# Feed-forward blocks that end by token half, and the norm behind them taken half by half

## The chip, the cores and the metric

One core of a Trainium2 chip runs the whole program. The metric is the time of one launch on the device, in microseconds; the kernel before was run three times, with a median of 3149.17 us (3148.85 to 3149.45). Besides, one execution was taken by the hardware profiler.

## The reference, cut to what matters

The model is a stack of layers on 256 tokens of width 1024. Two layers with a mixture of experts come first, then four layers whose second half is a plain feed-forward block. What is computed around the change is this, four times:

```python
def _layernorm(x, g, b):
    mu = mean(x); var = mean((x - mu) ** 2)
    return (x - mu) * rsqrt(var + eps) * g + b

def _swiglu(x, w_gate_up, w_down):           # hidden width 2816
    gate, up = split(x @ w_gate_up, 2)
    return (silu(gate) * up) @ w_down

for i in range(4):
    h = mixer_i(x)                            # HGRN, mLSTM, S5, HGRN
    x = _layernorm(ALPHA_2 * x + h, ...)
    x = _layernorm(ALPHA_2 * x + _swiglu(x, ...), ...)
```

A norm is taken over the 1024 values of one token. So the norm of the first 128 tokens needs nothing of the other 128.

## The kernel before, in words

Each engine has its own program, written out in order, and the engines meet at semaphores. The residual `h` lies in SBUF as two halves of 128 tokens (`t` = 0, 1), each of two column halves of 512 (`c` or `q` = 0, 1). `acc` is four PSUM banks, two for each token half: banks 4 and 5 for the first, 6 and 7 for the second. Before a feed-forward block, `residual_pe` has put the scaled residual there.

**The feed-forward block** (`glu_pe`, L559) has 11 parts of 256 hidden channels. For each part `glu_pe_up` (matmuls of L536 and L537) makes the gate and the up projection. ACT and DVE then make the hidden values of the part (`glu_act_step`, `glu_dve_step`): ACT copies the low product of "up" (L608), DVE adds it (L623), multiplies (L626), casts (L628) and takes the low part (L630), which announces `glu_hid_done`. Then `glu_pe_down` (L540, matmuls of L552) adds the part's product with the down weights to `acc`: 24 matmuls, 12 for the first token half and then 12 for the second. The hidden values are the operand that is loaded as weights. The down product of a part runs on PE one step late, behind the next part's up products, so that the hidden values are made under it. At the end, PE does up(10), down(9), down(10). In down(10) the first half's 12th matmul announces `glu_first_sum`, and the last matmul `glu_down_done`. The weights come through a ring of 12 slots that SP fills in order; a slot is loaded again when its use is announced.

**The norm behind it** is number 5, 7, 9 and 11 (`ln_dve`, L439, with `ALPHA` already in). DVE takes the statistics of the first half as soon as `glu_first_sum` is there (two of L452, then L455 and L457), then those of the second half when `glu_down_done` is there. ACT takes a square root for each half (`ln_act`, L475). Only then does DVE apply the norm: for each half a reciprocal (L462) and, for each column half, L465 and L468, the second of which announces `ln_done`.

**What follows norms 5, 7 and 9** is `turn_pe` (L361): four calls of a filler matmul on an idle operand (`keep_busy`, L359, two records each), then for each of the four pieces of `h` four transposes (L377) as soon as its `ln_done` is there, then five calls more of the filler. ACT copies each transposed piece (L407), but in its program this comes behind both square roots; DVE takes the low parts (L418, four), but behind the whole norm. Then ACT and DVE split the first two weight units of the next stage in the same way (L281 on ACT, then L286 on DVE), and PE begins the next projection: L2475 (the mLSTM's gates) behind norm 5, L312 behind norms 7 and 9. Behind norm 11 comes only the store of `h`.

Of the kernel before, what the change touches and what calls it, by code (L numbers as in the profile page):

```python
# [26 lines left out]
ALU = mybir.AluOpType  # L27
# [5 lines left out]
TT = T // P  # L33
# [61 lines left out]
def build(nc, W, out):  # L95

    ctx = ExitStack()
    with ctx:
# [3 lines left out]
        def sem(name):  # L102

            if name not in sems:
                sems[name] = ctx.enter_context(nc.semaphore(name))
            return sems[name]

        def sb(name, shape, dt=F32):
            return ctx.enter_context(nc.sbuf_tensor(name, shape, dt))

        def done(name):

            counts[name] = counts.get(name, 0) + 1
            return counts[name]


        act_step, dve_step, pool_step = sem("act_step"), sem("dve_step"), sem("pool_step")
        act_steps, dve_steps, pool_steps = Count(), Count(), Count()
# [6 lines left out]
        acc = psum[:, 4:8, :].rearrange("p (t b) n -> p t (b n)", t=TT)  # L125
# [43 lines left out]
        h = sb("h", [P, TT, D])  # L169
        ln_gb = scratch[:, SCR - 1, :].rearrange("p (k d) -> p k d", k=2)  # L170
# [57 lines left out]
        def slot_r(n):  # L228
            return ring_r[n % RING][:, :]
# [197 lines left out]
        mean_var = small[:, 24:28].rearrange("p (t s) -> p t s", t=TT)  # L427
        ln_sd = small[:, 28:30]
        ln_rstd = small[:, 30:32]
# [6 lines left out]
            pool.dma_start(ln_gb[:, 0, :], g.partition_broadcast(P)).then_inc(sem("ln_params_landed"), 16)  # L436
            pool.dma_start(ln_gb[:, 1, :], b.partition_broadcast(P)).then_inc(sem("ln_params_landed"), 16)

        def ln_dve(dve, n, alpha, wait_mix, mix=acc, by_tile=True):  # L439


            v = dve
            halves = [slice(c * 512, (c + 1) * 512) for c in range(2)]
            y = mix if alpha is None else h
            for t, c in [(t, c) for t in range(TT) for c in range(2)] if by_tile else [(t, c) for c in range(2) for t in range(TT)]:
                wait_mix(dve, t, c)
                x = y[:, t, halves[c]]
                if alpha is not None:
                    v.scalar_tensor_tensor(out=x, in0=x, scalar=alpha, in1=mix[:, t, halves[c]],
                                           op0=ALU.mult, op1=ALU.add).then_inc(dve_step, 1)  # L450
                    dve.wait_ge(dve_step, dve_steps.next())
                v.bn_stats(bn_s[:, t, c, :], x).then_inc(dve_step, 1)  # L452
                dve.wait_ge(dve_step, dve_steps.next())
                if c == 1:
                    v.bn_aggr(mean_var[:, t, :], bn_s[:, t, :, :]).then_inc(dve_step, 1)  # L455
                    dve.wait_ge(dve_step, dve_steps.next())
                    v.tensor_scalar(mean_var[:, t, 1:2], mean_var[:, t, 1:2], LN_EPS, None, ALU.add).then_inc(sem("ln_var"), 1)  # L457
                    dve.wait_ge(sem("ln_var"), done("ln_var"))
            dve.wait_ge(sem("ln_params_landed"), 32 * (n + 1))
            for t in range(TT):  # L460
                dve.wait_ge(sem("ln_sd_done"), 2 * n + t + 1)
                v.reciprocal(ln_rstd[:, t:t + 1], ln_sd[:, t:t + 1]).then_inc(dve_step, 1)  # L462
                dve.wait_ge(dve_step, dve_steps.next())
                for x in halves:
                    v.scalar_tensor_tensor(out=h[:, t, x], in0=y[:, t, x], scalar=mean_var[:, t, 0:1], in1=ln_gb[:, 0, x],  # L465
                                           op0=ALU.subtract, op1=ALU.mult).then_inc(dve_step, 1)
                    dve.wait_ge(dve_step, dve_steps.next())
                    v.scalar_tensor_tensor(out=h[:, t, x], in0=h[:, t, x], scalar=ln_rstd[:, t:t + 1], in1=ln_gb[:, 1, x],  # L468
                                           op0=ALU.mult, op1=ALU.add).then_inc(sem("ln_done"), 1)
                    dve.wait_ge(sem("ln_done"), done("ln_done"))  # L470

        def ln_act(act, n):
            for t in range(TT):
# [63 lines left out]
                        mm = pe.matmul(bank[:, 0:T], w[1][:, j, fc], both[:, 0, j, :], start=False, stop=(j == KT - 1))  # L537
                mm.then_inc(sem(name), 1)

        def glu_pe_down(pe, g, s, i=0):  # L540

            step = i * SLOTS + s
            pe.wait_ge(sem("glu_hid_done"), step + (g.g0 + 1))
            n, _ = g.unit("down", s, i)
            pe.wait_ge(sem("glu_down_split"), step + (g.g0 + 1))
            w = [x.rearrange("p (f n) -> p f n", f=FT) for x in (glu_hi["down"][s % 2], slot_r(n))]
            hid = [x.rearrange("p (f t) -> p f t", f=FT) for x in (hid_hi[s % 2], hid_lo[s % 2])]
            for t in range(TT):
                for c in range(2):
                    for f in range(FT):  # L550
                        for x, a in PASSES:
                            mm = pe.matmul(acc[:, t, c * 512:(c + 1) * 512], hid[x][:, f, t * P:(t + 1) * P],  # L552
                                           w[a][:, f, c * 512:(c + 1) * 512],
                                           start=False, stop=(s == g.n - 1 and f == FT - 1 and x == 1))
                if t == 0 and isinstance(s, int) and s == g.n - 1:
                    mm.then_inc(sem("glu_first_sum"), 1)
            mm.then_inc(sem("glu_down_done"), 1)

        def glu_pe(pe, g):  # L559
            glu_pe_up(pe, g, 0)  # L560
            glu_pe_up(pe, g, 1)
            glu_pe_down(pe, g, 0)
            with pe.Fori(0, g.loops) as i:
                for k in range(SLOTS):
                    glu_pe_up(pe, g, 2 + k, i)
                    glu_pe_down(pe, g, 1 + k, i)
            for s in range(2 + SLOTS * g.loops, g.n):
                glu_pe_up(pe, g, s)
                glu_pe_down(pe, g, s - 1)
            glu_pe_down(pe, g, g.n - 1)  # L570

        USED = {"gate": "glu_gate_ready", "up": "glu_up_ready", "down": "glu_down_done"}

# [73 lines left out]
        def glu_ahead_dve(dve, g):  # L647
            glu_low(dve, g, "gate", 0)
            glu_low(dve, g, "up", 0)
# [7 lines left out]
        def wait_glu(g):  # L657
            def wait(dve, t, c):
                if c == 0 and t == 0:
                    dve.wait_ge(sem("glu_first_sum"), g.nth + 1)  # L660
                elif c == 0:
                    dve.wait_ge(sem("glu_down_done"), g.g0 + g.n)
            return wait
# [1281 lines left out]
        def wait_experts(g):  # L1945
            return lambda dve, t, c: dve.wait_ge(sem("experts_done"), TT * g.layer + t + 1)
# [1230 lines left out]
        ffn = [None] * 4  # L3177
# [38 lines left out]
        def wait_out(stage):  # L3216
            return lambda dve, t, c: dve.wait_ge(sem(OUT_UNIT), plan[stage][1] - 2 + 2 * c)
# [126 lines left out]
        @block.vector  # L3344
        def _(dve):
            turn_parts_dve(dve, 0)
            dn_dve(dve)
            ln_dve(dve, 0, ALPHA_FIRST, wait_out("dn_out"), by_tile=False)
            route_dve(dve, 0)
            experts_dve(dve, moe[0])  # L3350
            ln_dve(dve, 1, None, wait_experts(moe[0]))
            turn_parts_dve(dve, 2)
            da_dve(dve)
            ln_dve(dve, 2, ALPHA_FIRST, wait_out("da_out"), by_tile=False)
            route_dve(dve, 1)
            experts_dve(dve, moe[1])
            ln_dve(dve, 3, None, wait_experts(moe[1]))
            turn_parts_dve(dve, HG_LN[0])
            hg_dve(dve, 0)
            glu_ahead_dve(dve, ffn[0])  # L3360
            ln_dve(dve, 4, ALPHA_SECOND, wait_out("hg0_out"), by_tile=False)
            turn_parts_dve(dve, 5)
            glu_dve(dve, ffn[0])
            ln_dve(dve, 5, None, wait_glu(ffn[0]))
            turn_parts_dve(dve, ML_TURN)
            ml_dve(dve)
            glu_ahead_dve(dve, ffn[1])
            ln_dve(dve, 6, ALPHA_SECOND, wait_out("ml_out"), by_tile=False)
            turn_parts_dve(dve, 7)
            glu_dve(dve, ffn[1])  # L3370
            ln_dve(dve, 7, None, wait_glu(ffn[1]))
            turn_parts_dve(dve, S5_TURN)
            s5_dve(dve)
            glu_ahead_dve(dve, ffn[2])
            ln_dve(dve, 8, ALPHA_SECOND, s5_mix_dve, s5_mix, by_tile=False)
            turn_parts_dve(dve, 9)
            glu_dve(dve, ffn[2])
            ln_dve(dve, 9, None, wait_glu(ffn[2]))
            turn_parts_dve(dve, HG_LN[1])
            hg_dve(dve, 1)  # L3380
            glu_ahead_dve(dve, ffn[3])
            ln_dve(dve, 10, ALPHA_SECOND, wait_out("hg1_out"), by_tile=False)
            turn_parts_dve(dve, 11)
            glu_dve(dve, ffn[3])
            ln_dve(dve, 11, None, wait_glu(ffn[3]))


# [14 lines left out]
```

## Time and profile before

| | us |
|---|---|
| median of 3 runs | 3149.17 (3148.85 to 3149.45) |
| the profiled execution's own time | 3146.78 |
| its span | 3145.2 |
| PE busy (matmul), DVE busy, ACT busy | 2857.0, 1557.1, 906.5 |
| granted TensorE clock, mean | 0.957 of full speed |

The span is the time from the first to the last instruction in the trace. Busy time is the sum of an engine's instructions; matmuls are pipelined, so PE is busy on paper also where matmuls overlap. The engines work side by side, so only what lies on the chain that ends last sets the time.

### The profile page before, as it was taken

To read this page: it belongs to the slowest core of one execution; us is meant where nothing else is said; L and a number is where in the kernel's file an instruction comes from. 1 tells how busy PE (TensorE), PEld (TensorE's weight loads), DVE (VectorE), ACT (ScalarE), POOL (GpSimd) and SP (SyncE) were. 2 spreads that over 40 slices of the span, in tenths; PEclk is the share of its full clock that TensorE was granted. 3 is DMA by queue.
4 is the path that set the end of the run, shared out by engine and by line. 5 is a ranking of instruction groups with operands and counts; after the bars stand their busy time and mean duration, and the time that the engine had idled before them with its cause. 6 is when DMAs were issued, how large, how long until landed. Compare 5 with 4: busy or idle time off the path is not lost.

```text
span 3145.2 us, 41647 instructions
## 1 busy us (share of the span) xinstructions
PE 2857.0 (91%) x16772; PEld 2103.6 (67%) x16774; DVE 1557.1 (50%) x2133; ACT 906.5 (29%) x1016; POOL 217.7 (7%) x309
## 2 busy tenths in 40 slices
PE   8888999998969999998898999999968899988998
PEld 8786444444846444443687887878856878787887
DVE  7855111111664111111576665675589576567664
ACT  4522110101431110110433443344330344333442
POOL 2001000000000000000021000000066000002000
PEclk9998999999978999999999999999978999999999
DMA  9204899999415999999432554345520245532450
GB/s 306 94 1 161 360 422 422 422 422 396 163 51 220 422 422 422 422 422 398 144 106 94 174 187 141 121 145 188 188 68 1 99 160 187 150 128 81 148 188 26
DMA packets 274118, 681.86 MB, mean 217 GB/s; under 512 B 10984, under 2 KB 207856, under 8 KB 223296
## 3 DMA queue, kind: packets, MB, share of 16 engines
q1 hardware_dynamic: 266080, 639.79, 54.8%
q0 software_dynamic: 7904, 40.19, 3.5%
q8 instruction: 96, 1.57, 0.2%
q14 instruction: 38, 0.31, 0.0%
HBM read 678.88 MB, written 1.05 MB: 216 GB/s over the span
## 4 chain that ended last, share of the span: by engine, by line
PE 60%; DVE 18%; DMA 17%; issue 2%; ACT 2%; SPq 0%; POOL 0%; DVEq 0%; ACTq 0%; POOLq 0%
DMA ring<-moe_w 16%; PE psum L536 11%; PE psum L1646 8%; PE psum L552 8%; PE psum L537 5%; PE psum L325 5%; PE psum L336 5%; PE psum L312 4%; PE psum L1671 3%; DVE ring_r L286 2%; PE psum L2210 1%; PE psum L1629 1%; DVE scratch L808 1%; PE psum L359 1%; DVE h L468 1%
## 5 line engine op out<-in xcount | busy, mean ns | idle before, releaser
L536 PE MATMUL psum<-scratch_r,scratch_r 128*128 128x512 f32 x1408 | 498.7, 398 | 1.7 <-DVE scratch_r L418 1.6
L1646 PE MATMUL psum<-ring,scratch 128*64 128x512 f32 x2016 | 450.2, 595 | 43.2 <-DMA ring<-moe_w 43.1
L537 PE MATMUL psum<-scratch_r,ring_r 128*128 128x256 f32 x1408 | 395.1, 281 | 0.0
L1646 PEld LDWEIGHTS psum<-ring,scratch 128*64 128x64 f32 x2016 | 146.6, 137 | 320.9 <-issue 317.0
L536 PEld LDWEIGHTS psum<-scratch_r,scratch_r 128*128 128x128 f32 x1408 | 264.5, 188 | 70.1 <-DVE scratch_r L418 5.0
L588 DVE TENSOR_TENSOR ring_r<-ring,scratch_r 128x2048 fp32r<-128x2048 f32 x132 | 294.8, 2286 | 19.4 <-ACT scratch_r L581 19.2
L286 DVE TENSOR_TENSOR ring_r<-ring,scratch_r 128x2048 fp32r<-128x2048 f32 x88 | 203.6, 2321 | 172.3 <-ACT scratch_r L281 171.0
L1845 DVE SCALAR_TENSOR_TENSOR hT_r<-psum,small,hT_r 128x512 fp32r<-128x512 f32 x66 | 46.5, 746 | 453.5 <-ACT hT_r L1784 453.5
L537 PEld LDWEIGHTS psum<-scratch_r,ring_r 128*128 128x128 f32 x1408 | 265.8, 189 | 1.4
L581 ACT CAST scratch_r<-ring 128x2048 fp32r<-128x2048 f32 x132 | 247.1, 1912 | 60.4 <-PE psum L552 60.2
L552 PE MATMUL psum<-scratch_r 128*128 128x512 f32 x704 | 225.2, 392 | 0.0
L312 PE MATMUL psum<-scratch_r,scratch_r 128*128 128x256 f32 x896 | 206.5, 288 | 8.3 <-DVE ring_r L286 8.3
L1671 PE MATMUL psum<-ring,scratch 128*64 128x512 f32 x960 | 211.1, 592 | 0.0
L281 ACT CAST scratch_r<-ring 128x2048 fp32r<-128x2048 f32 x88 | 166.8, 1903 | 104.0 <-PE psum L336 86.5
L1784 ACT ACTIVATE hT_r<-psum,small 128x512 fp32r<-128x512 f32 x66 | 41.7, 683 | 430.4 <-PE psum L1671 430.4
L312 PEld LDWEIGHTS psum<-scratch_r,scratch_r 128*128 128x128 f32 x896 | 157.2, 196 | 10.3 <-issue 10.3
L1671 PEld LDWEIGHTS psum<-ring,scratch 128*64 128x64 f32 x960 | 68.9, 137 | 137.0 <-issue 137.0
L1827 DVE TENSOR_TENSOR scratch<-scratch,psum 128x512 f32<-128x512 f32 x33 | 22.7, 688 | 265.7 <-ACT scratch L1777 265.7
L552 PEld LDWEIGHTS psum<-scratch_r 128*128 128x128 f32 x704 | 132.1, 188 | 29.3
L312 PE MATMUL psum<-hT_r,scratch_r 128*128 128x256 f32 x448 | 129.6, 289 | 16.1 <-DVE ring_r L286 15.2
L336 PE MATMUL psum<-scratch_r 128*128 128x256 f32 x448 | 121.0, 299 | 24.8 <-DVE scratch_r L903 19.1
L552 PE MATMUL psum<-ring_r,scratch_r 128*128 128x512 f32 x352 | 137.2, 390 | 0.0
(522 smaller groups left out, 4890.9 us busy)
## 6 DMA issues: line engine op xcount, KB each, us to landing
ring<-moe_w SPq DMA_DIRECT2D x372, 1024.0 KB, 20.5
ring<-ffn_w_gate_up SPq DMA_DIRECT2D x88, 1024.0 KB, 5.1
ring<-ffn_w_down SPq DMA_DIRECT2D x44, 1024.0 KB, 4.9
ring<-hgrn_w_in SPq DMA_DIRECT2D x32, 1024.0 KB, 5.5
scratch<-moe_w POOLq DMA_DIRECT2D x24, 1024.0 KB, 11.2
ring<-a_w_in SPq DMA_DIRECT2D x16, 1024.0 KB, 12.8
ring<-mlstm_w_in SPq DMA_DIRECT2D x12, 1024.0 KB, 5.2
ring<-kv_w SPq DMA_DIRECT2D x8, 1024.0 KB, 11.9
```

Source lines behind the costliest of these rows:

```text
L281: act.copy(hi, slot(n)).then_inc(sem("unit_high"), 1)
L286: dve.tensor_tensor(slot_r(n), slot(n), hi, ALU.subtract).then_inc(sem("unit_split"), 1)
L312: mm = pe.matmul(bank[:, c, :], w[:, j, c * P:(c + 1) * P], x[:, j, :], start=(j == 0 and m == 0), stop=(j == KT - 1 and m == len(terms) - 1))
L325: mm = pe.matmul(bank[:, t, :], x[:, j, t * P:(t + 1) * P], w[:, j, :], start=(j == 0 and m == 0), stop=(j == KT - 1 and m == len(terms) - 1))
L336: mm = pe.matmul(acc[:, t, i * COLS:(i + 1) * COLS], x[:, j, t * P:(t + 1) * P], w[:, j, :], start=(j == 0 and m == 0), stop=(j == KT - 1 ...
L536: pe.matmul(bank, w[0][:, j, fc], both[:, :, j, :], start=(j == 0), stop=False)
L537: mm = pe.matmul(bank[:, 0:T], w[1][:, j, fc], both[:, 0, j, :], start=False, stop=(j == KT - 1))
L552: mm = pe.matmul(acc[:, t, c * 512:(c + 1) * 512], hid[x][:, f, t * P:(t + 1) * P], w[a][:, f, c * 512:(c + 1) * 512], start=False, stop=( ...
L581: act.copy(glu_hi[kind][s % 2], slot(n)).then_inc(sem(f"glu_{kind}_high"), 1)
L588: dve.tensor_tensor(slot_r(n), slot(n), glu_hi[kind][s % 2], ALU.subtract).then_inc(sem(f"glu_{kind}_split"), 1)
L1646: mm = pe.matmul(psum[c, k, :], xg[:, j, c], ws[x][:, i, k, :], start=(j == 0), stop=(j == KT - 1))
L1671: mm = pe.matmul(psum[c, 2 + b, :], moe_hidT[:, 2 * half + a, c], ws[x][:, a, b * 512:(b + 1) * 512], start=(half == 0 and a == 0), stop=( ...
```

## The change

In all four feed-forward blocks PE no longer does the last two down products one behind the other. It does down(9) and down(10) for the first token half, then down(9) and down(10) for the second. `glu_pe_down` gets an argument `of` for this; it waits for the hidden values and the split weights at each call, as before. `glu_down_done` is announced once for each part, behind its second half. The norm's function is cut in two, and with `apart=True` (norms 5, 7, 9 and 11 only) DVE does statistics and application of the first half, then statistics and application of the second. No instruction that computes is added or removed, and ACT's program is unchanged.

```diff
-        def ln_dve(dve, n, alpha, wait_mix, mix=acc, by_tile=True):
+        def ln_dve(dve, n, alpha, wait_mix, mix=acc, by_tile=True, apart=False):
+            if apart:
+                for t in range(TT):
+                    ln_stats_dve(dve, n, alpha, wait_mix, mix, [(t, c) for c in range(2)])
+                    if t == 0:
+                        dve.wait_ge(sem("ln_params_landed"), 32 * (n + 1))
+                    ln_apply_dve(dve, n, mix if alpha is None else h, t)
+                return
...
-        def glu_pe_down(pe, g, s, i=0):
+        def glu_pe_down(pe, g, s, i=0, of=range(TT)):
...
-            for t in range(TT):
+            for t in of:
...
-            mm.then_inc(sem("glu_down_done"), 1)
+            if TT - 1 in of:
+                mm.then_inc(sem("glu_down_done"), 1)
...
             for s in range(2 + SLOTS * g.loops, g.n):
                 glu_pe_up(pe, g, s)
-                glu_pe_down(pe, g, s - 1)
-            glu_pe_down(pe, g, g.n - 1)
+                if s < g.n - 1:
+                    glu_pe_down(pe, g, s - 1)
+            for t in range(TT):
+                for s in (g.n - 2, g.n - 1):
+                    glu_pe_down(pe, g, s, of=(t,))
...
-            ln_dve(dve, 5, None, wait_glu(ffn[0]))
+            ln_dve(dve, 5, None, wait_glu(ffn[0]), apart=True)
```

`ln_stats_dve` and `ln_apply_dve` hold the instructions of the old body unchanged; norms 7, 9 and 11 are called in the same way.

## Rows read from the trace of the kernel before

**Rows 1.** The page: the chain that ended last, shares of the span by engine.

```profile
PE 60%; DVE 18%; DMA 17%; issue 2%; ACT 2%; SPq 0%; POOL 0%; DVEq 0%; ACTq 0%; POOLq 0%
```

**Rows 2.** Chain of waits behind block 0: start us, us, what.

```profile
1914.89 5.23 PE psum L552 x23
...
1929.48 5.99 PE psum L359 x10
1935.47 5.47 PE psum L2475 x48
```

**Rows 3.** Timeline of DVE, last block: start us, us, engine line op out<-in xcount [idle].

```profile
3123.78 0.69 DVE L630 TENSOR_TENSOR scratch_r<-scratch,scratch_r 128x512 fp32r<-128x512 f32 x1
3129.40 1.43 DVE L452 BATCH_NORM_STATS2 small<-psum 128x6 f32<-128x512 f32 x2 [4.93 <-PE psum L552]
...
3132.19 1.43 DVE L452 BATCH_NORM_STATS2 small<-psum 128x6 f32<-128x512 f32 x2 [0.92 <-PE psum L552]
...
3133.90 0.15 DVE L457 TENSOR_SCALAR small<-small 128x1 f32<-128x1 f32 x1
3134.09 0.16 DVE L462 RECIPROCAL small<-small 128x1 f32<-128x1 f32 x1
...
3136.64 0.75 DVE L468 SCALAR_TENSOR_TENSOR h<-h,small,scratch 128x512 f32<-128x512 f32 x1
...
3139.99 0.75 DVE L468 SCALAR_TENSOR_TENSOR h<-h,small,scratch 128x512 f32<-128x512 f32 x1
```

**Rows 4.** Timeline of ACT, last block.

```profile
3134.14 0.20 ACT L475 ACTIVATE small<-small 128x1 f32<-128x1 f32 x1 [2.64 <-DVE small L457]
```

**Rows 5.** Timeline of PE, last block's two down products.

```profile
3120.98 0.40 PE L552 MATMUL psum<-scratch_r 128*128 128x512 f32 x1
...
3123.53 0.61 PE L552 MATMUL psum<-scratch_r 128*128 128x512 f32 x2
...
3128.97 0.61 PE L552 MATMUL psum<-scratch_r 128*128 128x512 f32 x2
...
3131.70 0.39 PE L552 MATMUL psum<-scratch_r 128*128 128x512 f32 x1
```

**Rows 6.** Timeline of PE and DVE where PE waits for an operand (behind norm 6).

```profile
2087.90 2.87 DVE L418 TENSOR_TENSOR scratch_r<-psum,scratch_r 128x512 fp32r<-128x512 f32 x4
...
2090.82 0.50 PE L536 MATMUL psum<-scratch_r,scratch_r 128*128 128x512 f32 x1 [0.53 <-DVE scratch_r L418]
...
2091.16 0.28 PE L537 MATMUL psum<-scratch_r,ring_r 128*128 128x256 f32 x1
```

**Rows 7.** Timeline of PE behind norm 5.

```profile
1919.94 3.59 PE L359 MATMUL psum<-ident 128*128 128x512 f32 x8
...
1929.31 6.15 PE L359 MATMUL psum<-ident 128*128 128x512 f32 x10
```

**Rows 8.** Timeline of PE and DVE behind norm 7.

```profile
2284.50 1.12 PE L377 MATMUL psum<-ident,h 128*128 128x128 f32 x4 [0.92 <-DVE h L468]
...
2288.33 2.29 DVE L286 TENSOR_TENSOR ring_r<-ring,scratch_r 128x2048 fp32r<-128x2048 f32 x1 [0.98 <-ACT scratch_r L281]
```

**Rows 9.** Timeline of PE and DVE behind norm 9.

```profile
2729.59 1.12 PE L377 MATMUL psum<-ident,h 128*128 128x128 f32 x4 [0.61 <-DVE h L468]
...
2733.41 4.49 DVE L286 TENSOR_TENSOR ring_r<-ring,scratch_r 128x2048 fp32r<-128x2048 f32 x2 [0.98 <-ACT scratch_r L281]
...
2736.65 0.68 PE L312 MATMUL psum<-scratch_r,scratch_r 128*128 128x256 f32 x1
```

**Rows 10.** Windows: us, busy and count of PE, PEld, DVE, ACT, POOL; PEclk, DMA share, GB/s.

```profile
2082.40:2085.10 2.70, 1.27 (x10) 0.94 (x10) 2.56 (x5) 0.58 (x1) 0.00 (x0) 1.00 0.00 0
1923.50:1929.50 6.00, 2.69 (x18) 1.94 (x18) 5.71 (x9) 1.76 (x3) 0.44 (x1) 1.00 0.21 71
1929.30:1931.30 2.00, 2.00 (x5) 0.88 (x4) 1.90 (x4) 1.70 (x3) 0.52 (x3) 0.55 0.45 158
```

**Rows 11.** Timeline of SP's DMA issues.

```profile
1903.54 16.96 SPq L679 DMA_DIRECT2D ring<-mlstm_w_in  x4
```

More of the change, by code:

```diff
@@ L437, in ln_params, with ln_stats_dve @@
             pool.dma_start(ln_gb[:, 1, :], b.partition_broadcast(P)).then_inc(sem("ln_params_landed"), 16)
-        def ln_dve(dve, n, alpha, wait_mix, mix=acc, by_tile=True):
+        def ln_dve(dve, n, alpha, wait_mix, mix=acc, by_tile=True, apart=False):
[6 more added lines that the diff above has]
+                return
+            ln_stats_dve(dve, n, alpha, wait_mix, mix,
+                         [(t, c) for t in range(TT) for c in range(2)] if by_tile else [(t, c) for c in range(2) for t in range(TT)])
+            dve.wait_ge(sem("ln_params_landed"), 32 * (n + 1))
+            for t in range(TT):
+                ln_apply_dve(dve, n, mix if alpha is None else h, t)
+        def ln_stats_dve(dve, n, alpha, wait_mix, mix, order):
             v = dve
@@ L444, in ln_dve @@
             y = mix if alpha is None else h
-            for t, c in [(t, c) for t in range(TT) for c in range(2)] if by_tile else [(t, c) for c in range(2) for t in range(TT)]:
+            for t, c in order:
                 wait_mix(dve, t, c)
@@ L458, in ln_dve, with ln_apply_dve @@
                     dve.wait_ge(sem("ln_var"), done("ln_var"))
-            dve.wait_ge(sem("ln_params_landed"), 32 * (n + 1))
-            for t in range(TT):
-                dve.wait_ge(sem("ln_sd_done"), 2 * n + t + 1)
-                v.reciprocal(ln_rstd[:, t:t + 1], ln_sd[:, t:t + 1]).then_inc(dve_step, 1)
-                dve.wait_ge(dve_step, dve_steps.next())
[L464 to L470, printed above, removed]
+        def ln_apply_dve(dve, n, y, t):
+            v = dve
+            dve.wait_ge(sem("ln_sd_done"), 2 * n + t + 1)
+            v.reciprocal(ln_rstd[:, t:t + 1], ln_sd[:, t:t + 1]).then_inc(dve_step, 1)
+            dve.wait_ge(dve_step, dve_steps.next())
+            for x in (slice(c * 512, (c + 1) * 512) for c in range(2)):
+                v.scalar_tensor_tensor(out=h[:, t, x], in0=y[:, t, x], scalar=mean_var[:, t, 0:1], in1=ln_gb[:, 0, x],
+                                       op0=ALU.subtract, op1=ALU.mult).then_inc(dve_step, 1)
+                dve.wait_ge(dve_step, dve_steps.next())
+                v.scalar_tensor_tensor(out=h[:, t, x], in0=h[:, t, x], scalar=ln_rstd[:, t:t + 1], in1=ln_gb[:, 1, x],
+                                       op0=ALU.mult, op1=ALU.add).then_inc(sem("ln_done"), 1)
+                dve.wait_ge(sem("ln_done"), done("ln_done"))
         def ln_act(act, n):
@@ L547, in glu_pe_down @@
             hid = [x.rearrange("p (f t) -> p f t", f=FT) for x in (hid_hi[s % 2], hid_lo[s % 2])]
-            for t in range(TT):
+            for t in of:
                 for c in range(2):
@@ L568, in glu_pe @@
                 glu_pe_up(pe, g, s)
-                glu_pe_down(pe, g, s - 1)
-            glu_pe_down(pe, g, g.n - 1)
+                if s < g.n - 1:
+                    glu_pe_down(pe, g, s - 1)
+            for t in range(TT):
+                for s in (g.n - 2, g.n - 1):
+                    glu_pe_down(pe, g, s, of=(t,))
         USED = {"gate": "glu_gate_ready", "up": "glu_up_ready", "down": "glu_down_done"}
@@ L3370, in _ @@
             glu_dve(dve, ffn[1])
-            ln_dve(dve, 7, None, wait_glu(ffn[1]))
+            ln_dve(dve, 7, None, wait_glu(ffn[1]), apart=True)
             turn_parts_dve(dve, S5_TURN)
@@ L3377, in _ @@
             glu_dve(dve, ffn[2])
[L3378 removed]
+            ln_dve(dve, 9, None, wait_glu(ffn[2]), apart=True)
             turn_parts_dve(dve, HG_LN[1])
@@ L3384, in _ @@
             glu_dve(dve, ffn[3])
-            ln_dve(dve, 11, None, wait_glu(ffn[3]))
+            ln_dve(dve, 11, None, wait_glu(ffn[3]), apart=True)
 def kernel(**inputs):
```

## The prediction

> **What bounds the kernel now.** I read the page's chain first: 60% of it is PE, 18% DVE, 17% DMA [rows 1]. The engines take turns, so I ask at each end of a feed-forward block who hands over to whom. The chain of waits behind block 0 shows it: PE's down products, then DVE's norm alone from 1920.2 to 1928.8, the transposes, then PE's fillers and the gates' projection [rows 2]. So the norm lies bare on the path, four times. The timeline of the last block prices it. PE's last down matmul starts at 3131.70 and takes 0.39 [rows 5], so it ends at 3132.09. DVE starts the second statistics at 3132.19 and ends the norm at 3139.99 + 0.75 = 3140.74 [rows 3]. Of these 8.55 us, 3134.09 to 3137.43 is the application of the FIRST half (its last L468 ends at 3137.39, and 0.04 goes to the next start), whose sum was ready since 3129.40. That is 3.34 us that could have run under PE.
>
> **PE: the added wait.** One down matmul comes every 0.228 us: from the first start, 3120.98, to the 48th, 3131.70, are 47 steps [rows 5]. Before, all 24 matmuls of down(9) hid the making of the last hidden values; now only 12 do. The 12th and 13th start within the group at 3123.53, the 13th at 3123.76 [rows 5]. The 13th will now be the first of down(10), and needs the hidden values, which DVE finishes at 3123.78 + 0.69 = 3124.47 [rows 3]. Where PE waits on DVE, it starts 0.05 after DVE's end (2087.90 + 2.87 = 2090.77, PE at 2090.82), and its next matmul comes 0.34 later instead of 0.23, since the weight load is bare [rows 6]. So down(10) starts at 3124.52 and is 0.11 late on top: as if at 3124.63. The stall is 0.87 us. Bounds: 0.7 (the wait without that 0.11) to 1.3 (if the whole first matmul of 0.50 [rows 6] were bare). Behind the stalled instruction is queued everything that PE has left, 36 matmuls, so PE's end moves in full, to 3132.96. The second call of each part waits on nothing new.
>
> The row shows 0.11 for the bare weight load. The Trainium skill (TensorE: Matmul & The Clock Gate, Part 2, LDWEIGHTS) says that PE can pull a weight load ahead of matmuls in flight. By that the stall would be 0.76 us and the four ends together 0.4 us shorter. Here the operand loaded is itself what is awaited, so I keep the row.
>
> **DVE: the first half.** Down(10)'s 12th matmul started at 3128.97 before [rows 5], and DVE began 0.43 later, at 3129.40 [rows 3]. Now it starts at 3124.63 + 11 x 0.228 = 3127.14, and DVE begins at 3127.57. Statistics take 3132.19 to 3134.05, 1.86 us [rows 3]. Then comes a wait that was hidden: ACT's square root starts 0.09 after the variance (3134.14 against 3134.05) and takes 0.20 [rows 4]; with some 0.03 back to DVE and less the 0.04 that stood there already, it adds 0.28. Bounds 0.2 to 0.4. Nothing but DVE's own next step is queued behind it. The reciprocal starts at 3127.57 + 1.86 + 0.32 = 3129.75, and the application takes 3.30: done at 3133.05. PE ends at 3132.96, so the second half's statistics could start at 3133.05 (0.09 after PE, as before). The two meet: the first half hides just fully. If it is late by x, x is paid once.
>
> **DVE: the second half.** 3133.05 + 1.86 + 0.32 + 3.31 = 3138.54, against 3140.74: **2.20 us less** at each end. In terms: -3.34 (application hidden) + 0.87 (PE's stall) + 0.28 (bare square root) = -2.19.
>
> **Behind the norm.** ACT copies the first half's transposed pieces only after the second square root, at 3135.3, still before the second half's pieces come; DVE takes the four low parts behind the whole norm as before. So both keep their place relative to the last `ln_done`. PE's fillers (8 records in 3.59 us [rows 7]) start at its own end, 0.87 later, and end 3.6 later at 3136.4; the first half's transposes follow at once, and the second half's last piece is ready at 3138.5. The fillers don't delay it.
>
> The three inner ends gain more, because of the clock. Before, between the fillers and the last transposes PE had little to do for 6 us: 2.69 us busy in 1923.5 to 1929.5, and then the clock was granted at 0.55 [rows 10], close to the lower of its two levels (1.2 of 2.4 GHz). The ten filler records behind it start at 1929.31, and the gates follow at about 1934.9 to 1935.5 [rows 2, 7]; at the rate of the first eight (0.43 us) they would take 4.3 of these 5.6 us. Now the fillers end at PE's end + 3.4 and the last transposes start at its end + 5.6: about 2.8 us of little work. A stretch of 2.7 us like it, with 1.27 us of PE, kept 1.00 behind norm 6 [rows 10]. I take the clock to hold. Then:
> - behind norm 5 the fillers bound PE: 2.2 + 1.3 = **3.5 us**;
> - behind norm 7 the chain is transposes, ACT's copy and cast, DVE's split (2288.33 [rows 8]). The last transposes took 1.12 at the low clock against 0.66 at the full one: 2.2 + 0.46 = **2.7 us**;
> - behind norm 9 the last transposes start at 2729.59 and the projection at 2736.65 [rows 9], PE-bound by the fillers. At the full clock they would be through 0.5 + 4.3 after the transposes' start, at 2732.2 with the shift. But the first split then decides: half of 4.49 from 2733.41 ends at 2735.66 [rows 9], less 2.2 and 0.46: 2733.0. From 2736.65 to 2733.05: **3.6 us**;
> - behind norm 11: **2.2 us**.
>
> Sum 12.0 us. The profiled execution took 3146.78 with a span of 3145.2; its forecast is 3134.8. The median is 2.4 above that execution, so I predict 3149.2 - 12.0 = **3137.2 us**.
>
> **What costs nothing.** The slot of down(9) comes free later: the part's last matmul now starts at 3124.63 + 23 x 0.228 = 3129.9 instead of 3126.2, by 3.6 us; the last slot's by 0.87. SP issues them in order, and the four last loads run from 1903.54 to 1920.50 [rows 11]. They hold the 11th and 12th unit of the next stage, behind ten others, and PE only starts that stage at 1935 [rows 2]. Without that cover, up to 3.6 us would come back at three places. DVE reads the first half's banks while PE writes the other two; it did so for the statistics too, with the same 1.43 for the pair under PE's matmuls (3129.40) as after them (3132.19) [rows 3].
>
> **Rivals.**
> 1. The clock falls behind the norms as before, or at two of three places. Then each end gives only 2.2: 4 x 2.2 = 8.8, **3140.4 us**. For it: the drop came at the three places after similar but not equal times, so where it strikes seems chance; against it, the row with 2.7 us. Chance 0.27.
> 2. The inner gains are given back: the stage behind is held by something that the norm doesn't move, a weight load or parameters. Only the last end remains: **3147.0 us**, no change. For it: DMA is 17% of the chain [rows 1]. Against: no DMA stands in the chain from the norm to the gates [rows 2], and ACT, DVE and PE all start from `h`. Chance 0.09.
> 3. Slower: PE's new stall drops the clock under the 36 matmuls that follow. At the lower level each costs 0.228 more, 8.2 us an end; four ends give 32.8 - 8.8 = +24, **3173 us**. It decides from ten slow matmuls an end on. Against: 0.87 us is a third of the stretch that kept 1.00 [rows 10]. Chance 0.02; smaller losses of this side, such as a first half that comes more than 2.2 us late to the second, 0.02.
> 4. The change doesn't do what it says: DVE's first application starts only behind `glu_down_done`. Its program and the semaphores exclude it; its time would be 3149.2 + 4 x (0.87 + 0.28) = 3153.8. Chance 0.01.
>
> **How the numbers follow.** The forecast has 0.59, and its own range is 3135 to 3139: the stall's and the square root's bounds give -0.3 to +0.6 us at four ends, the fillers' rate 1 us, and the chain's "issue" (2% [rows 1], some 60 us, by where the program's instructions lie) may shift by 1 or 2. The range to 8 in 10 takes in rival 1 and the way to it, and as much below for a larger gain where the stages behind start at another moment: **3134.0 to 3144.0**. A measurement of this kernel can tell 0.2% from no change, 6.3 us: faster is below 3142.9. The forecast and nearly all of rival 1 lie there: 0.86. Same 0.10, slower 0.04.
>
> **What would show it.** At each end, the 13th down matmul behind the last up product starts 0.7 to 0.9 later than the rate gives. DVE's first L465 runs while PE still multiplies, its fourth ends within 0.2 of PE's end, and from PE's last matmul to the last L468 pass 5.6 us instead of 8.65. Each L462 comes about 0.3 behind its L457. Behind norms 5, 7 and 9 the clock stays at 1.00 and the ten filler records take 4.4 us. The prediction is wrong if the stall is over 1.5 us, if DVE is still at the first half when PE has ended, or if a stage behind has the old length plus what its norm gained.

## The result, and the profile after

The changed kernel took 3136.22 us (median of 7 runs, 3135.70 to 3141.61); the kernel before, measured beside it, 3149.29 us (7 runs, 3147.86 to 3152.40). The ratio is 0.9961, with a 95% interval of 0.9950 to 0.9973: faster by 0.4%, clear of no change. (The ratios here and below are estimated from all executions, so they differ a little from the quotient of the two medians.) The forecast was 3137.2 in a range of 3134.0 to 3144.0. The profiled execution has a span of 3133.6 us, against 3145.2 before.

PE's timeline of the changed kernel's last block answers to [rows 5] (L568 is the down product's line now, L552 before):

```profile
3111.23 0.40 PE L568 MATMUL psum<-scratch_r 128*128 128x512 f32 x1
...
3113.79 0.39 PE L568 MATMUL psum<-scratch_r 128*128 128x512 f32 x1
3114.78 0.50 PE L568 MATMUL psum<-scratch_r 128*128 128x512 f32 x1 [0.60 <-DVE scratch_r L650]
3115.12 0.39 PE L568 MATMUL psum<-ring_r,scratch_r 128*128 128x512 f32 x1
...
3122.85 0.39 PE L568 MATMUL psum<-scratch_r 128*128 128x512 f32 x1
```

The 12th matmul starts at 3113.79, so the 13th was due at 3114.02. It starts at 3114.78, released by DVE's last hidden step, and its follower comes 0.34 later instead of 0.23. The stall is 0.76 + 0.11 = 0.87 us. From the first down matmul to PE's end it is 12.01 us, against 11.11 before, 0.90 more.

DVE and ACT at the same end, in answer to [rows 3, 4] (L466 statistics, L471 variance, L478 reciprocal, L481 and L484 the application; on ACT L491 the square root):

```profile
3114.03 0.69 DVE L650 TENSOR_TENSOR scratch_r<-scratch,scratch_r 128x512 fp32r<-128x512 f32 x1
3117.84 1.43 DVE L466 BATCH_NORM_STATS2 small<-psum 128x6 f32<-128x512 f32 x2 [3.11 <-PE psum L568]
...
3119.55 0.15 DVE L471 TENSOR_SCALAR small<-small 128x1 f32<-128x1 f32 x1
3120.07 0.16 DVE L478 RECIPROCAL small<-small 128x1 f32<-128x1 f32 x1 [0.37 <-ACT small L491]
...
3122.62 0.75 DVE L484 SCALAR_TENSOR_TENSOR h<-h,small,scratch 128x512 f32<-128x512 f32 x1
3123.41 1.43 DVE L466 BATCH_NORM_STATS2 small<-psum 128x6 f32<-128x512 f32 x2
...
3125.12 0.15 DVE L471 TENSOR_SCALAR small<-small 128x1 f32<-128x1 f32 x1
3125.67 0.16 DVE L478 RECIPROCAL small<-small 128x1 f32<-128x1 f32 x1 [0.40 <-ACT small L491]
3126.06 0.75 DVE L481 SCALAR_TENSOR_TENSOR h<-psum,small,scratch 128x512 f32<-128x512 f32 x1 [0.22 <-DVE small L478]
...
3128.41 0.75 DVE L484 SCALAR_TENSOR_TENSOR h<-h,small,scratch 128x512 f32<-128x512 f32 x1
```

```profile
3125.37 0.20 ACT L491 ACTIVATE small<-small 128x1 f32<-128x1 f32 x1 [5.43 <-DVE small L471]
```

The first half's application now runs at 3120.07 to 3123.37, under PE's matmuls, and ends 0.13 after PE's end at 3123.24. The second statistics start at 3123.41 with no idle time before them: DVE is just the bound. Each reciprocal waits some 0.4 us for ACT. The end comes at 3129.16, 5.92 us after PE's, where 8.65 passed before.

What follows an inner end, in answer to [rows 7 to 9]; three fences, PE behind norm 5, then PE and DVE behind norm 7, then behind norm 9:

```profile
1927.86 0.66 PE L377 MATMUL psum<-ident,h 128*128 128x128 f32 x4 [0.92 <-DVE h L484]
1928.35 4.46 PE L359 MATMUL psum<-ident 128*128 128x512 f32 x10
1932.25 0.68 PE L2495 MATMUL psum<-hT_r,scratch_r 128*8 128x256 f32 x1
```

```profile
2279.42 0.66 PE L377 MATMUL psum<-ident,h 128*128 128x128 f32 x4 [0.92 <-DVE h L484]
2282.78 4.49 DVE L286 TENSOR_TENSOR ring_r<-ring,scratch_r 128x2048 fp32r<-128x2048 f32 x2 [0.52 <-ACT scratch_r L281]
2285.22 0.36 PE L312 MATMUL psum<-hT_r,scratch_r 128*128 128x256 f32 x1 [0.85 <-DVE ring_r L286]
```

```profile
2720.86 0.66 PE L377 MATMUL psum<-ident,h 128*128 128x128 f32 x4 [0.92 <-DVE h L484]
2721.36 4.46 PE L359 MATMUL psum<-ident 128*128 128x512 f32 x10
2726.67 0.36 PE L312 MATMUL psum<-scratch_r,scratch_r 128*128 128x256 f32 x1 [0.85 <-DVE ring_r L286]
```

The ten filler records take 4.46 us each time, where they took 6.15, 5.69 and 6.72; the last transposes take 0.66, where behind norms 7 and 9 they took 1.12. PE behind norm 9 before:

```profile
2730.49 6.72 PE L359 MATMUL psum<-ident 128*128 128x512 f32 x10
```

In the changed kernel the fillers still hold PE behind norm 5; behind 7 and 9 PE waits for the split. The windows of the changed kernel behind norm 5, first around the transposes and then under the later fillers, show the clock at full (columns as in [rows 10]):

```profile
1925.30:1928.30 3.00, 1.98 (x17) 1.50 (x15) 2.86 (x5) 1.76 (x3) 0.20 (x1) 1.00 0.50 162
1928.30:1932.30 4.00, 4.00 (x13) 1.85 (x11) 3.66 (x8) 3.66 (x4) 0.56 (x3) 1.00 0.35 131
```

From such rows I measure each end in one way, free of what happened earlier: from the start of the first of the 48 down matmuls to the first projection matmul of the next stage (behind norm 11, to the end of the last L484).

| us | behind 5 | behind 7 | behind 9 | behind 11 | sum against before |
|---|---|---|---|---|---|
| before | 25.90 | 26.09 | 26.89 | 19.76 | |
| after | 22.38 | 23.65 | 23.62 | 17.93 | -11.1 |
| after, second profile | 22.39 | 23.61 | 23.61 | 17.94 | -11.1 |

An end up to the end of its norm repeats to 0.05 us from profile to profile. Behind it, where the clock has fallen, the length depends on when it fell: in the kernel before, the same ten fillers took 5.69 to 6.72 us. There is one profile of the kernel before, so I estimate from these fillers that the clock's part of the 11.1 us is known to about 1 us only.

### The profile page after: what moved, and what is told of

Read it like the earlier page. It is cut to its first block, busy times and chain, and to the rows that moved or that the text cites. A ratio compares the mean times of both kernels' runs of the same rounds, so it can differ in the third digit from the quotient of the medians.

```text
span 3133.6 us, 41657 instructions
## 1 busy us (share of the span) xinstructions
PE 2855.3 (91%) x16774; PEld 2103.7 (67%) x16774; DVE 1556.8 (50%) x2133; ACT 906.5 (29%) x1016; POOL 217.4 (7%) x309
## 4 chain that ended last, share of the span: by engine, by line
PE 58%; DVE 19%; DMA 18%; ACT 2%; issue 2%; SPq 0%; POOL 0%; DVEq 0%; ACTq 0%; POOLq 0%
DMA ring<-moe_w 17%; PE psum L552 11%; PE psum L1666 8%; PE psum L568 7%; PE psum L553 5%; PE psum L325 5%; PE psum L336 5%; PE psum L312 4%; PE psum L1691 3%; DVE ring_r L286 2%; PE psum L2230 1%; PE psum L1649 1%; DVE scratch L828 1%; DVE h L484 1%; DVE h L481 1%
## 5 line engine op out<-in xcount | busy, mean ns | idle before, releaser
L552 PE MATMUL psum<-scratch_r,scratch_r 128*128 128x512 f32 x1408 | 498.7, 398 | 2.1 <-DVE scratch_r L418 2.1
L552 PEld LDWEIGHTS psum<-scratch_r,scratch_r 128*128 128x128 f32 x1408 | 264.5, 188 | 70.4 <-DVE scratch_r L418 5.4
L568 PE MATMUL psum<-scratch_r 128*128 128x512 f32 x704 | 226.3, 392 | 2.4 <-DVE scratch_r L650 2.4
L312 PE MATMUL psum<-scratch_r,scratch_r 128*128 128x256 f32 x896 | 206.5, 288 | 9.2 <-DVE ring_r L286 9.1
L312 PEld LDWEIGHTS psum<-scratch_r,scratch_r 128*128 128x128 f32 x896 | 157.5, 196 | 11.8 <-issue 11.8
L568 PEld LDWEIGHTS psum<-scratch_r 128*128 128x128 f32 x704 | 132.1, 188 | 33.4 <-DVE scratch_r L650 4.1
L312 PE MATMUL psum<-hT_r,scratch_r 128*128 128x256 f32 x448 | 130.2, 291 | 16.4 <-DVE ring_r L286 15.5
L568 PE MATMUL psum<-ring_r,scratch_r 128*128 128x512 f32 x352 | 137.3, 390 | 0.0
```

The lines of the kernel that those rows point to most:

```text
L312: mm = pe.matmul(bank[:, c, :], w[:, j, c * P:(c + 1) * P], x[:, j, :], start=(j == 0 and m == 0), stop=(j == KT - 1 and m == len(terms) - 1))
L552: pe.matmul(bank, w[0][:, j, fc], both[:, :, j, :], start=(j == 0), stop=False)
```

## The experiments

Nine runs. The two medians of the changed kernel differ by 1.2 us, single executions of it by up to 6 and of the kernel before by up to 10. So the table of ends carries the verdicts, and the medians only confirm them.

**PE's new order alone.** The changed kernel, with every `apart=True` taken out:

```diff
-            ln_dve(dve, 5, None, wait_glu(ffn[0]), apart=True)
+            ln_dve(dve, 5, None, wait_glu(ffn[0]))
```

> The changed order of PE (last two down parts by token half), but the norm as before: statistics of both halves, then both applications. Theory (the gain is the first half's application under PE, the price is PE's stall): each end is 0.87 us LATER than before, since the second statistics follow PE's end and both applications come behind it; from the first of the 48 down matmuls to the last L468/L484 20.6 us (before 19.76, after 17.93). The clock behaves as before, since the stretch between fillers and last transposes keeps its 6 us. Time: before + 3.5 us, 3152.8. Rival (the order of PE alone brings the gain, e.g. through the clock or the slot that comes free at another moment): below 3145.

Measured: 3152.22 us (10 runs; before 3149.03), ratio 1.0006 (0.9997 to 1.0016): not told apart from no change by the time. DVE at the last end:

```profile
3137.39 1.43 DVE L466 BATCH_NORM_STATS2 small<-psum 128x6 f32<-128x512 f32 x2 [3.64 <-PE psum L568]
...
3145.19 0.75 DVE L484 SCALAR_TENSOR_TENSOR h<-h,small,scratch 128x512 f32<-128x512 f32 x1
```

The first down matmul starts at 3125.27, so the norm ends 20.67 us after it, 0.91 later than before, and so at all four places (0.91 to 0.94): the stall in full, and nothing for it. Ends: 26.62, 26.81, 26.99, 20.67. The third is only 0.1 longer, because the ten fillers there took 5.76 us instead of 6.72: the clock fell at another moment. The rival falls.

**The norm by halves alone.** The changed kernel with PE's old order:

```diff
                 glu_pe_up(pe, g, s)
-                if s < g.n - 1:
-                    glu_pe_down(pe, g, s - 1)
-            for t in range(TT):
-                for s in (g.n - 2, g.n - 1):
-                    glu_pe_down(pe, g, s, of=(t,))
+                glu_pe_down(pe, g, s - 1)
+            glu_pe_down(pe, g, g.n - 1)
```

> PE in the old order (24 matmuls of down(9), then 24 of down(10)), but the norm taken half by half. Theory: no stall of PE; but the first half's sum is there only 2.75 us before PE's end, so DVE is at the first half's application when PE ends: 1.43+0.4 statistics, 0.36 for the bare square root, 3.3 application, then 1.86 + 0.36 + 3.3 for the second half. From the first of the 48 down matmuls: 8.42 + 5.5 + 5.5 = 19.5 us, against 19.76 before: 0.3 us less at each end, 1 us in all, 3148. If the clock holds behind the norms it is not because of this change: the last transposes still come over 5 us after the fillers' end. Rival (DVE's order is what brings the gain, PE's order nothing): the full 12 us, 3137.

Measured: 3147.83 us (10 runs), ratio 0.9993 (0.9984 to 1.0003). DVE at the last end:

```profile
3130.11 1.43 DVE L466 BATCH_NORM_STATS2 small<-psum 128x6 f32<-128x512 f32 x2 [4.93 <-PE psum L568]
...
3135.68 1.43 DVE L466 BATCH_NORM_STATS2 small<-psum 128x6 f32<-128x512 f32 x2
...
3140.69 0.75 DVE L484 SCALAR_TENSOR_TENSOR h<-h,small,scratch 128x512 f32<-128x512 f32 x1
```

PE's last matmul ends at 3132.80; the second statistics start 2.9 us after it, behind the first application. Ends: 25.89, 25.88, 25.89, 19.75, together 1.2 us less. Only 0.4 of this is the norm, which ends 0.01, 0.20, 0.20 and 0.01 earlier (expected: 0.3 each). The rest stands behind norm 9, where the ten fillers took 4.94 us instead of 6.72:

```profile
2731.68 4.94 PE L359 MATMUL psum<-ident 128*128 128x512 f32 x10
```

So up to the end of the norms PE's order alone costs 3.7 us at the four places, DVE's order alone gains 0.4, and both together gain 7.7: the order on PE makes the time that the order on DVE uses. Over the whole ends the three figures are 2.5 us more, 1.2 less and 11.1 less, with the clock in each of them.

**The kernel before, with fillers in the gaps.** This tests whether the clock paid what the inner ends gained beyond the norm:

```diff
                     mm.then_inc(psum_ready, 1)
+                    if n in (6, 8, 10) and (t, q) != (1, 1):
+                        keep_busy(pe, psum[:, 4, :], 1)
```

> The kernel before, with one more call of the filler (two records, 0.86 us) behind each of the first three transposed pieces after norms 5, 7 and 9, in the gaps of 0.9 to 1.1 us where PE waits for the next piece. Norm and down products as before. Theory (the inner ends gained beyond 2.2 us because the clock held): the clock stays at 1.00, the ten filler records behind the last transposes take 4.4 instead of 5.6 to 6.7 us, and the kernel gains 1.3 + 0.5 + 1.4 = 3.2 us, 3146. Rival (the clock's fall costs nothing on the path, the rest of the gain has another source): 0, 3149.2; if the added fillers delay transposes, up to +1.

Measured: 3144.67 us (10 runs), ratio 0.9989 (0.9979 to 0.9998). PE behind norm 5, and the window of the transposes behind norm 7:

```profile
1928.52 1.02 PE L359 MATMUL psum<-ident 128*128 128x512 f32 x2
1929.60 0.65 PE L377 MATMUL psum<-ident,h 128*128 128x128 f32 x4
1930.09 4.46 PE L359 MATMUL psum<-ident 128*128 128x512 f32 x10
```

```profile
2278.50:2284.20 5.70, 4.97 (x22) 2.42 (x22) 5.42 (x9) 1.75 (x3) 0.00 (x0) 1.00 0.23 80
```

Ends: 24.21, 25.63, 25.63, 19.76: 1.7, 0.5 and 1.3 less, 3.4 in all, with norm and down products untouched. So holding the clock is worth 3.4 us against this profile of the kernel before.

**The changed kernel without the first fillers.**

```diff
-                keep_busy(pe, bank_of(f"turn{n}", "hT", 0), 6 if n % 2 else 4)
+                keep_busy(pe, bank_of(f"turn{n}", "hT", 0), 0 if n in (6, 8, 10) else 6 if n % 2 else 4)
```

> The changed kernel without the four filler calls ahead of the transposes behind norms 5, 7 and 9. Between the last down matmul and the last transposes PE then has 6 us with little to do instead of 2.8. Theory: the clock falls again at all or most of the three places, the last transposes take 1.1 instead of 0.66 and the ten filler records 5.6 to 6.7 instead of 4.46 us: the inner ends lose 1.3, 0.5 and 1.4, 3139.4 in all. Nothing else changes, since the fillers ended before the transposes that mattered. Rival (clock not decisive): as the changed kernel, 3136.2.

Measured: 3139.14 us (7 runs), ratio 0.9969 (0.9957 to 0.9980). PE behind norm 7, and the windows behind norms 5 and 7 under the ten filler records:

```profile
2282.51 1.12 PE L377 MATMUL psum<-ident,h 128*128 128x128 f32 x4 [0.92 <-DVE h L484]
2283.42 6.95 PE L359 MATMUL psum<-ident 128*128 128x512 f32 x10
```

```profile
1928.70:1932.70 4.00, 4.00 (x7) 1.70 (x6) 3.24 (x7) 3.66 (x4) 0.11 (x1) 0.50 0.41 131
...
2283.40:2287.40 4.00, 4.00 (x7) 1.71 (x6) 2.95 (x4) 3.65 (x3) 4.00 (x3) 0.50 0.40 60
```

The clock falls at all three places. Ends: 25.15, 25.10, 24.07, 17.93; the inner ones lose 4.7 us together, 2.8, 1.5 and 0.4, since the fillers took up to 6.95 us. The norms end as in the changed kernel (+17.94, 17.75, 17.75). The expectation of 3.2 us was right in kind, short by 1.5 us in size. That the median, 3139.14, still came as forecast (3139.4) doesn't confirm the size: the profile is 1.3 us shorter than the changed kernel's between the ends.

**The changed kernel again**, unaltered.

> The changed kernel again, unaltered, for a second profile of it and for the spread of its times. Theory: the spans of the ends repeat to 0.1 us (17.7 to 17.95 us from the first of the 48 down matmuls to the last L484); the stages between them vary by a microsecond either way; 3136.2, single executions up to 3141.6.

Measured: 3137.38 us (5 runs, 3135.68 to 3140.52; before 3149.19), ratio 0.9961 (0.9948 to 0.9975). Its ends stand in the table above. Its profiled execution has a span of 3137.5, and all of the 3.9 us against the first profile lie ahead of block 0's end: the first of the 48 down matmuls starts at 1913.81 instead of 1909.87, and from there to the end of the span it is 1223.7 us in both. They open earlier, between 1467 and 1541 us: the same matmul of L1649 starts 0.5 us later at 1467.3 and 1.2 later at 1468.1, one of L312 3.4 later at 1540.5. In that stretch the second profile was granted less of the clock; the window from 1465 to 1545, first of the first profile, then of the second:

```profile
1465.00:1545.00 80.00, 64.45 (x342) 40.17 (x343) 32.06 (x49) 21.87 (x27) 3.36 (x7) 0.94 0.65 237
1465.00:1545.00 80.00, 63.40 (x310) 38.98 (x311) 32.06 (x49) 20.92 (x25) 3.33 (x7) 0.89 0.67 242
```

**PE's stall filled.** Three matmuls of down(9)'s second half go ahead of down(10)'s first half; `cf` is a new argument with the column half and channel block:

```diff
-            for t in range(TT):
-                for s in (g.n - 2, g.n - 1):
-                    glu_pe_down(pe, g, s, of=(t,))
+            glu_pe_down(pe, g, g.n - 2, of=(0,))
+            glu_pe_down(pe, g, g.n - 2, of=(1,), cf=((0, 0),))
+            glu_pe_down(pe, g, g.n - 1, of=(0,))
+            glu_pe_down(pe, g, g.n - 2, of=(1,), cf=((0, 1), (1, 0), (1, 1)))
+            glu_pe_down(pe, g, g.n - 1, of=(1,))
```

> The changed kernel with three of down(9)'s matmuls for the second half (first column half, first 128 hidden channels) moved ahead of down(10) for the first half, into PE's stall. Theory: the stall of 0.87 us shrinks to about 0.2 and PE ends 0.7 earlier; but down(10)'s first half ends no earlier than now, as its start is set by the hidden values, so DVE is the bound: the second statistics start right behind the first application, at most 0.08 us earlier than now. Gain per end 0 to 0.1 us, 3136.2 to 3136.0. Rival (the stall is what the ends still pay): 0.7 us less at each, 2.8 us, 3133.4.

Measured: 3137.76 us (6 runs), ratio 0.9965 (0.9953 to 0.9977). PE's first and last down matmul, then DVE, at the last end:

```profile
3112.96 0.40 PE L567 MATMUL psum<-scratch_r 128*128 128x512 f32 x1
...
3123.90 0.39 PE L567 MATMUL psum<-scratch_r 128*128 128x512 f32 x1
```

```profile
3124.36 0.75 DVE L484 SCALAR_TENSOR_TENSOR h<-h,small,scratch 128x512 f32<-128x512 f32 x1
3125.14 1.43 DVE L466 BATCH_NORM_STATS2 small<-psum 128x6 f32<-128x512 f32 x2
```

PE ends 0.67 us earlier (11.33 instead of 12.01 after its first), and every end keeps its length to 0.04: 22.39, 23.61, 23.61, 17.94. PE's end is not what the changed kernel pays for any more; DVE is. What the filling removes is PE's idle time, not the wait for the hidden values: down(10)'s first half starts when it did, and DVE's norm hangs on that. What earlier hidden values would bring was not tried.

**And the last step put off.** On top of it, the first half's second `L484` goes behind the second statistics:

```diff
+                ln_stats_dve(dve, n, alpha, wait_mix, mix, [(0, c) for c in range(2)])
+                dve.wait_ge(sem("ln_params_landed"), 32 * (n + 1))
+                ln_apply_dve(dve, n, y, 0, last=False)
+                ln_stats_dve(dve, n, alpha, wait_mix, mix, [(1, c) for c in range(2)])
+                ln_scale_dve(dve, 0, slice(512, 1024))
+                ln_apply_dve(dve, n, y, 1)
```

> As the one with the filled stall, and DVE puts off the last step of the first half (its second L484) until the second half's statistics are done. Theory: the second statistics start 0.75 us earlier, PE being ready for them, and the put-off step of 0.79 us covers the second square root (0.36 us bare now): 0.5 us less at each end, 2 us in all, 3134.2. Rival (DVE's second statistics still wait for PE, or a transposed piece comes late because its L484 does): 0 or a loss.

Measured: 3136.03 us (5 runs), ratio 0.9958 (0.9944 to 0.9971). DVE at the last end (L468 statistics, L478 the step put off, L486 reciprocal):

```profile
3127.84 1.43 DVE L468 BATCH_NORM_STATS2 small<-psum 128x6 f32<-128x512 f32 x2
...
3129.74 0.75 DVE L478 SCALAR_TENSOR_TENSOR h<-h,small,scratch 128x512 f32<-128x512 f32 x1
3130.52 0.16 DVE L486 RECIPROCAL small<-small 128x1 f32<-128x1 f32 x1
```

The second reciprocal no longer waits. Ends: 21.88, 23.29, 23.29, 17.42: 1.7 us less in all by the trace (expected 2). Against the changed kernel the times can't tell it apart.

**Fewer fillers behind the transposes**, on the changed kernel:

```diff
-                keep_busy(pe, psum[:, 4, :], 5)
+                keep_busy(pe, psum[:, 4, :], 3 if n in (6, 8, 10) else 5)
```

> The changed kernel with three filler calls instead of five behind the last transposes of norms 5, 7 and 9. Theory (behind norm 5 the fillers bind, behind 7 and 9 the first unit's split): the gates behind norm 5 start about 1 us earlier, behind norms 7 and 9 nothing moves, and the clock still holds: 1 us in all, 3135.3. Rival (the fillers are what holds the clock there): PE waits 2.6 us for the split behind norms 7 and 9 and the clock falls under the projection: +1 to +3 us.

Measured: 3136.06 us (5 runs; before 3148.13), ratio 0.9961 (0.9948 to 0.9975). PE behind norms 5 and 7, in two fences, and the window of the projection behind norm 7:

```profile
1931.45 0.28 PE L2495 MATMUL psum<-hT_r,scratch_r 128*8 128x256 f32 x1 [0.35 <-DVE scratch_r L2628]
```

```profile
2284.67 0.35 PE L312 MATMUL psum<-hT_r,scratch_r 128*128 128x256 f32 x1 [2.57 <-DVE ring_r L286]
```

```profile
2284.70:2286.70 2.00, 2.00 (x11) 2.00 (x12) 2.00 (x2) 0.53 (x1) 0.02 (x1) 0.57 1.11 174
```

Both were half right. The end behind norm 5 shrinks to 21.58 (0.8 less) and now waits for DVE; behind 7 and 9 it stays (23.61, 23.62). But there PE is idle for 2.57 us, and the clock falls under the projection, 0.3 us after its start behind norm 7 (granted 0.57 in the window shown) and 1.2 us after it behind norm 9: the rival's fall of the clock. What it costs doesn't show in the time: from block 0's first of the 48 down matmuls to the span's end it is 1223.9 us, 1223.7 in the changed kernel.

**A further version.** On top of the put-off step: three filler calls instead of five, and the first weight unit of the S5 and of the second HGRN stage split ahead of the norm (norm 7 is shown; norm 9 is done in the same way):

```diff
+            unit_high(act, plan["s5_in"])
             norm(7)
...
+            unit_low(dve, plan["s5_in"])
             ln_dve(dve, 7, None, wait_glu(ffn[1]), apart=True)
```

> A version built on what the runs so far showed. On top of the filled stall and the put-off step: ACT casts the next stage's first weight unit behind its last feed-forward copy, and DVE takes its low part in the 3 us in which it waits for the first half's sum (norms 7 and 9 only; the S5 and the second HGRN stage); and behind norms 5, 7 and 9 three filler calls follow the last transposes instead of five. Theory: behind norms 7 and 9 the first projection no longer waits for the split that ends 5.9 us behind the norm, but for the low parts of h (2.9) and three fillers (0.5 + 2.6): 2.7 us less at each; behind norm 5 the fillers end 1.7 earlier and the gates wait for the low parts, 1.0 less. With the 0.3 to 0.5 of each end that the put-off step gave, 6.4 + 1.7 = 8 us below the changed kernel, 3129. Rival 1 (the split delays the first statistics or lands in their way): the ends take longer than 17.42 us. Rival 2 (with fewer fillers the clock falls): the stages' first projections run at the low clock and the gain is gone, 3136.

Measured: 3132.88 us (5 runs, 3128.51 to 3133.16), ratio 0.9945 (0.9931 to 0.9958). DVE, then PE, at the end behind norm 7:

```profile
2269.01 2.28 DVE L286 TENSOR_TENSOR ring_r<-ring,scratch_r 128x2048 fp32r<-128x2048 f32 x1
2272.20 1.43 DVE L468 BATCH_NORM_STATS2 small<-psum 128x6 f32<-128x512 f32 x2 [0.92 <-PE psum L574]
```

```profile
2283.58 2.74 PE L359 MATMUL psum<-ident 128*128 128x512 f32 x6
2285.99 0.45 PE L312 MATMUL psum<-hT_r,scratch_r 128*128 128x256 f32 x1
```

The split fits into DVE's wait with 0.92 us to spare, and the projection follows the fillers at the full clock (granted 1.00 at 2286 to 2288). Ends: 21.07, 20.40, 20.38, 17.43, together 8.3 us less than after, as expected. The median is 3.3 to 4.5 us below the two of the changed kernel, not 8: from the first down matmul of block 0 to the span's end the profile shows 1217.2 against 1223.7, 6.5 less, so about 1.8 came back in the stages between; and block 0's end came late in this execution, at 1914.10. It beats the kernel before clearly. Against the changed kernel the two intervals just overlap, but all its 5 executions (up to 3133.16) lie below the lowest of the 12 of the changed kernel (3135.68), and below those of the version with fewer fillers, measured beside it (from 3135.11).

## Why the prediction was right

- **The application hidden under PE (-3.34 an end):** right: 3.30 us of it now run before PE's end or within 0.13 of it. The two sides met as worked out: PE's end at +12.01 after its first down matmul (forecast 11.98), the second statistics at +12.18 (12.07).
- **PE's stall (+0.87):** measured 0.87, and PE's end moved by 0.90. Alone it costs 0.91 an end (PE's order alone). But PE's late end was no cost once DVE was the bound: filling 0.67 us of it changed nothing. The sum still has the 0.87, because the wait for the hidden values delays the first half's sum, and with it DVE, by as much: it is right as a step and misleading as a price for PE's end. The weight load was bare, 0.34 us to the next matmul as in [rows 6]; the Trainium skill's rule of loads pulled ahead (TensorE: Matmul & The Clock Gate, Part 2, Step-by-step, LDWEIGHTS) does not show where the load itself is awaited.
- **The bare square root (+0.28):** measured 0.33 for the first half and 0.36 for the second (0.52 and 0.55 from variance to reciprocal, 0.19 before). At the ends behind norms 5 and 11, 0.2 us more stands between reciprocal and L481, which I had no row for.
- **Each end 2.20 less:** measured 1.83, 1.98, 2.02 and 1.83, from 19.76 and 19.77 to 17.93, 17.79, 17.75 and 17.93. Too high by 0.2 to 0.4: the sizes of the last point, and 0.1 for the second statistics, which start at +12.18 instead of +12.07. The prediction's -0.3 to +0.6 us "at four ends" is what its bounds give at one end; at four they give -1.0 to +2.2, and the measured miss, 4 x 2.20 - 7.7 = 1.1 us, lies outside the first and inside the second.
- **Behind the norm:** forecast 3.5, 2.7, 3.6 and 2.2, measured 3.52, 2.44, 3.27 and 1.83. In 3.52 stand 1.83 of the norm (forecast 2.2) and 1.69 of the clock (forecast 1.3): the two misses cancel, so this hit to 0.02 us is luck. Behind norms 7 and 9 the clock's part was 0.46 and 1.25 (forecast 0.5 and 1.4). The two experiments on the fillers show the clock's share from both sides: held in the kernel before it gives 3.4 us, let fall in the changed one it costs 4.7 at the ends. How much it is depends on when the clock falls, and no row told that ahead. It held at all three places in all six profiles that keep the short stretch, and fell at all three in before, in both runs with one half of the change, and in the one without the first fillers. The stretch that the prediction put at 2.8 us, from the last of the first fillers to the first of the later ones, measures 2.9 to 3.1 in the changed kernel and up to 3.7 where the stall is filled. (The first fillers end 3.43 us after PE's end, as the prediction's 3136.4 has it; its "3.6 later" doesn't add up to that.) The reason I gave (a like stretch behind norm 6 [rows 10]) was one row, and the run with fewer fillers shows how near it was: there 2.57 us of true idleness were followed by the fall. The transposes stand in the short stretch and break it up; that this is what held it was not tried by itself.
- **The sum of 12.0:** the ends give 11.1. The rest of the median's 13.1 is what the stages between and ahead of the ends do from run to run. Between the ends both profiles of the changed kernel are 1.4 us shorter than before (from block 0's first of the 48 down matmuls to the span's end 1223.7 us, before 1236.2, of which 11.1 at the ends); ahead of them they are 0.87 and 4.8 longer. The 1.4 us mean nothing: over all eleven profiles the stages between the ends take 1133.3 to 1139.2 us, and they are the shortest and the longest in kernels that change nothing there. I count 11 us as the change's. That the median came within 1 us of 3137.2 is in part luck, then: the ends gave 0.9 us less than the sum, the scatter 2 us more.
- **At no cost:** the slots that come free later, and DVE in PSUM under PE's matmuls. L466 takes 1.43 and L481 0.75 there as before. The four loads behind block 0 run for 17.86 us instead of 16.96, and PE still waits for no load in the first 58 us of the stage behind, only for its splits, 2.9 us in all, as before.
- **Rivals:** the falling clock (3140) and the slower one (3173) are excluded by the windows and the ends' table; given back later (3147) by the time from block 0's end to the span's end, 12.4 us less; without effect (3154) by DVE's first reciprocal, which comes 3 us ahead of PE's end. Neither half of the change could have been left out: 3152 and 3148.

## What to carry to other kernels

Where one engine finishes a long sum and another then works alone on its parts, order the sum by the parts that the second engine wants, and check that both changes come together: each by itself gave next to nothing here. The right amount of work behind the first part's sum is what the second engine needs for it; here 24 matmuls, 5.5 us, against 5.5 us of norm. And read a stretch behind such an end for the granted clock too: a shorter gap can pay again what the gap itself saved.

## What the runs showed of the hardware

- Where 5.8 to 6.9 us with nothing but transposes on PE (2.7 us busy in the 6 us of [rows 10]) lay between the large matmuls, the clock fell to about half ahead of the fillers that followed or under them, at twelve of twelve places in four profiles. Where 2.9 to 3.7 us with the same transposes lay there, it stayed at 1.00, at eighteen of eighteen places in six profiles. Behind 2.57 us of no work at all, which followed six filler records (2.74 us), it fell under the next projection, at two of two places in one profile.
- Where PE had waited for DVE to make the operand that is loaded as weights, its matmul started 0.05 to 0.06 us after DVE's end ([rows 6], the changed kernel's last end), and the next one came 0.34 us later instead of 0.23.
- Ahead of block 0's end executions differ by some 4 us: its first down matmul (of the last 48) starts at 1909.0 to 1910.1 us in seven profiles and at 1913.8 to 1914.7 in four, with the same kernel in both groups. Between the two profiles of the changed kernel, 3 of these 4 us open between 1467 and 1541 us, where one was granted 0.94 of the clock and the other 0.89. Why the clock fell more often there was not looked for.
- Between the second half's reciprocal, which had waited for ACT, and the L481 behind it 0.2 us more passed behind norms 5 and 11 and none behind 7 and 9, in each profile where DVE waits so. Behind the first half's reciprocal, which waits as well, it passed nowhere. It went when the wait went (the put-off step). The cause stays open.
